# Hybrid decoder block on one core: the second norm's rows are turned by VectorE in 32x32 squares instead of by TensorE

## The chip, the core and the metric

The kernel runs on one core of a Trainium2 chip. The core has five engines, each with its own in-order stream of instructions: TensorE (PE: matrix products, with PEld for its weight loads), VectorE (DVE), ScalarE (ACT), GpSimd (POOL) and SyncE (SP), which here issues nearly all DMAs. Engines wait for one another, and for DMAs, by semaphores. The metric is the time of one execution on the device in microseconds; lower is better. In three runs the kernel before took 1904.53, 1905.38 and 1905.64 us, so its median is 1905.38 us.

## The reference, cut to what matters

One decoder layer on x of shape (1, 2048, 1024), all in float32:

```
h    = rmsnorm(x, norm_mix);  proj = h @ w_in            # 1024 x 2048
y    = concat(rmsnorm(rg_lru(conv4(...)) * gelu(...)), rmsnorm(silu(layernorm(conv31(...)))))
x    = x + y @ w_out
h    = rmsnorm(x, norm_ffn)                              # the second norm
f    = silu(h @ w_gate) * (h @ w_up)                     # hidden width 2816
x    = x + f @ w_down
out  = rmsnorm(x, norm_final)
```

The change concerns the line `h = rmsnorm(x, norm_ffn)` and how its result reaches the products with w_gate and w_up. TensorE contracts over the partition axis, so h, which is computed with positions on the partitions, must be turned so that its 1024 channels lie on the partitions.

## The kernel before, in words

Precision: every float32 operand is split in a high part (`_hi`) and a rest (`_lo`), and each product is three matmuls (lines 2133 to 2135): hi by hi, lo by hi, hi by lo. The split is a cast by ACT followed by a subtraction, by POOL for some operands and by DVE for others.

Stage 1 (to about 425 us) does the first norm, the input projection, the convolutions and the recurrence. It is not touched.

Stage 2, the **row steps** (425 to 624 us): 16 steps w = 0 to 15, each for 128 positions. In step w TensorE makes the output projection: four products `ps[e]` of twelve matmuls (`wo_hi`, `y_hi`, ...), 48 in all. Between them come a few short matmuls for the norms of later positions. DVE adds the four results to the residual in `row[w % 4]` (`add_row`, line 1729). ACT then takes the row's mean square and its root (`row_std`, lines 1351 and 1352), and DVE scales the row to `hn[w % 2]` (`row_scaled`, lines 1896 and 1903). PE, a little later, turns `hn` with eight 128x128 transposes into the banks 6 and 7 (`turn_h2`, line 2312); ACT copies them to `h2t` (`h2_copy`, line 1346), and SP stores `h2t` in the DRAM scratch `h2_scr` (`store_h2`, line 550), whose layout is channel by position. SP stores the row itself in `x2_scr` and loads later residuals and later y. The operand y of step w + 1 is cast by ACT (`y_split`, line 1260) and its rest is made by POOL (`y_lo_part`, line 888); PE's step waits for it (`pe.wait_ge(s_ylo, w + 1)`).

Stage 3 computes gate and up products by Strassen-like sums, for the first half of the positions (h = 0) and then for the second. Its left operands are seven tiles a0 to a6 (`a_raw`, split in `a_hi` and `a_lo`), each [128, 4 x 512]. For h = 0 four of them are loaded from `h2_scr` in row steps 9 and 10, and the others are sums made by DVE (`first_half_sum`, line 1874) in row steps 11 and 12. For step 14 POOL's program reads: the rest of y for step 14, the rest `b_lo` of the first weight matrix, a wait for the fourth sum (`s_sum0 >= 4`), the rest `a_lo` of a0, and only then the rest of y for step 15. The **hidden steps** i = 0 to 10 each take two weight matrices (m = 2i for gate, 2i + 1 for up), with seven products of twelve matmuls per matrix, n = 1, 2, 3, 4, 5, 0, 6. Product 2 waits for the rest `t_lo` of the matrix's sums by POOL, product 3 for DVE's sum `sum11` (line 1943). In hidden step i `sum11` of the gate matrix overwrites a part of the tile `gt`, and so it waits until operand 3 of step i - 1 (`f_scr<-gt`, line 685) is stored: `dve.wait_ge(s_fst[2], 16 * i)`. Operands of the down projection go to `f_scr`. For the second half SP loads parts of `h2_scr` into `quad` in the hidden steps 1, 3, 5 and 7, and POOL makes sums of them (`quad_sums`, line 987) in front of `t_lo` in its stream.

Stage 4 is the down projection; at its end DVE and ACT do the final norm on 16 row tiles `x2[t]`, and SP stores them.

The order of all this is written by hand, as tables of the step at which each piece stands (`TURNED`, `LOAD_AT`, `SUM_AT`, ...).

## Time and profile before

| | |
|---|---|
| median of three runs | 1905.38 us |
| the profiled execution, span of its instructions | 1902.7 us |
| PE busy | 1875.1 us, 99% |
| POOL, DVE, ACT busy | 60%, 58%, 42% |
| DMA | 284.20 MB, mean 149 GB/s |
| TensorE clock granted | full in all 40 slices |

The span is that of one execution; the timed median lies 2.7 us above it. Durations of matmuls in the profile overlap: 12 matmuls with a duration of 0.39 us each follow one another every 0.227 us. So PE's progress is read from start times, not from durations. The last row step, 15, ends at 624.1 us.

### The profile page before, as it was taken

Reading aid. Unit: us, or ns where it says so; the run is one execution under the profiler, and the core shown is the slowest. Engines: PE = TensorE matmul, PEld = TensorE weight load, DVE = VectorE, ACT = ScalarE, POOL = GpSimd, SP = SyncE. Lnnn points to the kernel's source line nnn. Section 1 sums busy time; section 2 is a strip of 40 time slices with the busy share of each in tenths; the row PEclk is TensorE's granted clock in tenths of the full one; section 3 lists DMA queues with packets and bytes.
Section 4 is the critical chain, followed back from the end, with each engine's and each line's share of the span. In section 5 each row is a group of like instructions: output and inputs, shape, how many; then the busy total and the mean of one; then the engine's idle time right before and its main releaser. Section 6 shows DMA issues by size and latency. Waiting matters only on the chain.

```text
span 1902.7 us, 22499 instructions
## 1 busy us (share of the span) xinstructions
PE 1875.1 (99%) x8374; PEld 1544.2 (81%) x8374; DVE 1106.6 (58%) x1269; ACT 808.4 (42%) x938; POOL 1144.9 (60%) x427
## 2 busy tenths in 40 slices
PE   9999999999999999999999999999999999999998
PEld 7888788877788788888888788888888888888886
DVE  6899988997645755455545854445443025433535
ACT  6466766585643533333333433333333222232235
POOL 3577477945734465666655755555555676676663
PEclk9999999999999999999999999999999999999999
DMA  6222132265777334533355433323333765655455
GB/s 196 78 79 88 45 100 78 75 224 172 247 240 231 117 125 127 153 119 127 112 153 176 151 105 114 106 88 105 115 105 127 288 225 190 210 189 211 166 198 221
DMA packets 240946, 284.20 MB, mean 149 GB/s; under 512 B 12095, under 2 KB 166207, under 8 KB 240364
## 3 DMA queue, kind: packets, MB, share of 16 engines
q1 hardware_dynamic: 240874, 283.25, 44.8%
q8 instruction: 45, 0.74, 0.2%
q14 instruction: 25, 0.20, 0.0%
q10 hardware_dynamic: 2, 0.00, 0.0%
HBM read 200.90 MB, written 82.31 MB: 149 GB/s over the span
## 4 chain that ended last, share of the span: by engine, by line
PE 82%; POOL 6%; DVE 5%; ACT 2%; issue 2%; DMA 2%; POOLq 0%; SPq 0%; DVEq 0%; ACTq 0%
PE ps L2133 19%; PE ps L2135 19%; PE ps L2134 19%; PE acc L2133 8%; PE acc L2135 8%; PE acc L2134 8%; DVE a_lo L1863 1%; POOL nsq L877 1%; PE ps L2161 1%; DVE t_sum L1887 1%; POOL nsq L879 1%; POOL w_lo L804 1%; POOL f_lo L1018 0%; DVE wo_lo L1707 0%; POOL glu L827 0%
## 5 line engine op out<-in xcount | busy, mean ns | idle before, releaser
L933 POOL TENSOR_TENSOR t_lo<-t_sum,t_hi 128x2048 fp32r<-128x2048 f32 x44 | 205.6, 4674 | 165.3 <-ACT t_hi L1366 165.2
L927 POOL TENSOR_TENSOR b_lo<-m_raw,b_hi 128x1536 fp32r<-128x1536 f32 x44 | 157.6, 3582 | 179.2 <-ACT b_hi L1361 121.9
L1018 POOL TENSOR_TENSOR f_lo<-f_raw,f_hi 128x2048 fp32r<-128x2048 f32 (+1 forms) x42 | 182.2, 4338 | 129.3 <-ACT f_hi L1518 124.8
L2133 PE MATMUL ps<-h_hi,w_hi 128*128 128x512 f32 x512 | 201.1, 393 | 0.8 <-POOL w_lo L804 0.8
L2135 PE MATMUL ps<-h_hi,w_lo 128*128 128x512 f32 x512 | 199.4, 389 | 0.0
L2134 PE MATMUL ps<-h_lo,w_hi 128*128 128x512 f32 x512 | 199.2, 389 | 0.0
L1887 DVE TENSOR_TENSOR t_sum<-m_raw 128x512 f32<-128x512 f32 x88 | 141.7, 1630 | 97.4 <-PE acc L2135 87.6
L1518 ACT CAST f_hi<-f_raw 128x2048 fp32r<-128x2048 f32 (+1 forms) x42 | 74.3, 1769 | 263.6 <-PE ps L2135 168.1
L2133 PE MATMUL ps<-wd_hi,f_hi 128*128 128x512 f32 x462 | 179.8, 389 | 0.8 <-POOL wd_lo L1025 0.8
L2134 PE MATMUL ps<-wd_lo,f_hi 128*128 128x512 f32 x462 | 179.7, 389 | 0.0
L2135 PE MATMUL ps<-wd_hi,f_lo 128*128 128x512 f32 x462 | 179.7, 389 | 0.0
L2076 DVE TENSOR_TENSOR wd_raw<-wd_raw 128x1024 f32<-128x1024 f32 (+1 forms) x30 | 73.6, 2453 | 174.8 <-DMA wd_raw<-in_w_down 174.8
L2133 PE MATMUL ps<-a_hi,t_hi 128*128 128x512 f32 x440 | 171.5, 390 | 0.8 <-DVE p5s L1959 0.8
L2134 PE MATMUL ps<-a_lo,t_hi 128*128 128x512 f32 x440 | 171.2, 389 | 0.0
L2135 PE MATMUL ps<-a_hi,t_lo 128*128 128x512 f32 x440 | 171.2, 389 | 0.0
L2133 PEld LDWEIGHTS ps<-h_hi,w_hi 128*128 128x128 f32 x512 | 96.1, 188 | 20.8 <-POOL w_lo L804 1.2
L2135 PEld LDWEIGHTS ps<-h_hi,w_lo 128*128 128x128 f32 x512 | 96.1, 188 | 20.3
L2134 PEld LDWEIGHTS ps<-h_lo,w_hi 128*128 128x128 f32 x512 | 96.2, 188 | 19.6 <-issue 0.2
L2133 PE MATMUL acc<-a_hi,t_hi 128*128 128x512 f32 x264 | 103.7, 393 | 4.0 <-DVE gt L1959 2.4
L2133 PE MATMUL ps<-a_hi,b_hi 128*128 128x512 f32 x264 | 102.9, 390 | 4.2 <-DVE a_lo L1863 2.6
L2133 PE MATMUL ps<-wo_hi,y_hi 128*128 128x512 f32 x256 | 104.6, 409 | 2.3 <-DVE wo_lo L1707 1.0
L2134 PE MATMUL acc<-a_lo,t_hi 128*128 128x512 f32 x264 | 103.3, 391 | 0.0
(257 smaller groups left out, 4689.1 us busy)
## 6 DMA issues: line engine op xcount, KB each, us to landing
f_raw<-f_scr SPq DMA_DIRECT2D x35, 1024.0 KB, 4.9
wd_raw<-in_w_down SPq DMA_DIRECT2D x60, 512.0 KB, 6.6
f_scr<-fs SPq DMA_DIRECT2D x110, 256.0 KB, 2.1
m_raw<-in_w_gate SPq DMA_DIRECT2D x88, 256.0 KB, 3.9
m_raw<-in_w_up SPq DMA_DIRECT2D x88, 256.0 KB, 5.1
w_raw<-in_w_in SPq DMA_DIRECT2D x32, 512.0 KB, 5.3
f_scr<-gt SPq DMA_DIRECT2D x44, 256.0 KB, 2.0
xt<-in_x SPq DMA_DIRECT2D x16, 512.0 KB, 6.3
```

The lines of the kernel that those rows point to most:

```text
L804: g.tensor_tensor(w_lo[q % 2][:, :, :, :], w_raw[q % 2][:, :, :, :], f32(w_hi[q % 2][:, :, :, :]), ALU.subtract).then_inc(s_wlo, 1)
L877: g.tensor_tensor(into[:, 0:2], source[:, 0:2], source[:, 2:4], ALU.add).then_inc(s_fold, 1)
L879: g.tensor_tensor(into[:, 0], into[:, 0], into[:, 1], ALU.add).then_inc(s_fold, 1)
L927: g.tensor_tensor(b_lo[b][:, :, :, :], m_raw[b][:, 0:3], f32(b_hi[b][:, :, :, :]), ALU.subtract).then_inc(s_mlo, 1)
L933: g.tensor_tensor(t_lo[b][:, :, :, :], t_sum[b][:, :, :, :], f32(t_hi[b][:, :, :, :]), ALU.subtract).then_inc(s_mlo, 1)
L1018: g.tensor_tensor(f_lo[j % 3][:, 0:n], f_raw[j % 2][:, 0:n], f32(f_hi[j % 3][:, 0:n]), ALU.subtract).then_inc(s_dlo, 1)
L1518: a.copy(f_hi[j % 3][:, 0:n], f_raw[j % 2][:, 0:n]).then_inc(s_dhi, 1)
L1887: v.tensor_tensor(into, in0, in1, ALU.subtract).then_inc(s_t, 1)
L2076: v.tensor_tensor(raw[:, 0, 0:c1 - c0], raw[:, 0, 0:c1 - c0], raw[:, 1, 0:c1 - c0], WD[m][2]).then_inc(s_t, 1)
L2133: pe.matmul(bank, lhs[0](c), rhs[0](c), start=first, stop=False, skip_group_check=more)
L2134: pe.matmul(bank, lhs[0](c), rhs[1](c), start=False, stop=False, skip_group_check=more)
L2135: mm = pe.matmul(bank, lhs[1](c), rhs[0](c), start=False, stop=last, skip_group_check=more)
```

## The change

- The 128 transposes of PE and the 32 copies of ACT are gone, and so are the tiles `h2t`.
- DVE turns each scaled row in its place in the stream: one instruction for [128, 32 squares of 32] turns every 32x32 square in itself (`row_turned`). It writes to `turned[g]`, one tile for a group of four rows. In `turned` the partition says the position within a square's 32 and the channel within its 32, mixed by the squares' order, so positions within a block of 512 stand in another order from here on.
- `hn` has four buffers for rows 0 to 3.
- SP stores a group of four rows with four DMAs of 32 partitions each, 512 KB in runs of 512 bytes, at row steps 7, 9 and 12. The last group is halved: rows 12 and 13 at step 14, and rows 14 and 15 in hidden step 0, each with four DMAs of 256 KB in runs of 256 bytes (64 positions).
- The first half's quarters are loaded with four DMAs of 32 partitions each, in row steps 10 and 11 (before 9 and 10), and the sums stand in row steps 12 and 13 (before 11 and 12).
- The second half is copied in DRAM from `h2_scr` to the new scratch `h2n_scr` in hidden step 1 (four DMAs, 4 MB in all), and SP waits for the copies to land before it issues the first `quad` load.
- The rows' other order is undone where rows are loaded and stored: `x2` loads and `out` stores become four DMAs of 32 partitions each. Of the last four pieces two are issued by ACT.

On DVE, before, the sums of a1 to a6 (`a_raw<-a_raw`) around row steps 11 to 13:

```order
L1903 SCALAR_TENSOR_TENSOR hn_208<-row_188,rstd,g_row 128x1024
L1874 TENSOR_TENSOR a_raw_62<-a_raw_65,a_raw_66 128x2048
L1874 TENSOR_TENSOR a_raw_65<-a_raw_61,a_raw_65 128x2048
L1729 SCALAR_TENSOR_TENSOR row_185<-ps,rms,row_185 128x512 x4
L1896 RECIPROCAL rstd<-rstd 128x1
L1903 SCALAR_TENSOR_TENSOR hn_207<-row_185,rstd,g_row 128x1024
L1874 TENSOR_TENSOR a_raw_63<-a_raw_62,a_raw_61 128x2048
L1874 TENSOR_TENSOR a_raw_64<-a_raw_60,a_raw_63 128x2048
L1729 SCALAR_TENSOR_TENSOR row_186<-ps,rms,row_186 128x512 x4
```

On DVE, now, the same sums, around row steps 12 to 14 (`row_187` is the row of step 12):

```order
L1768 SCALAR_TENSOR_TENSOR row_187<-ps,rms,row_187 128x512 x4
L1937 RECIPROCAL rstd<-rstd 128x1
L1944 SCALAR_TENSOR_TENSOR hn_209<-row_187,rstd,g_row 128x1024
L1955 STREAM_TRANSPOSE turned_148<-hn_209 128x32x32
L1915 TENSOR_TENSOR a_raw_62<-a_raw_65,a_raw_66 128x2048
L1915 TENSOR_TENSOR a_raw_65<-a_raw_61,a_raw_65 128x2048
L1768 SCALAR_TENSOR_TENSOR row_188<-ps,rms,row_188 128x512 x4
L1937 RECIPROCAL rstd<-rstd 128x1
L1944 SCALAR_TENSOR_TENSOR hn_210<-row_188,rstd,g_row 128x1024
L1955 STREAM_TRANSPOSE turned_148<-hn_210 128x32x32
L1915 TENSOR_TENSOR a_raw_63<-a_raw_62,a_raw_61 128x2048
L1915 TENSOR_TENSOR a_raw_64<-a_raw_60,a_raw_63 128x2048
```

Each pair of sums now stands one row step later and behind a square transpose. POOL's order is the same in both kernels; there, around row step 14, it is:

```order
L888 TENSOR_TENSOR y_lo_168<-y_raw_156,y_hi_162 128x1024
L927 TENSOR_TENSOR b_lo_78<-m_raw_74,b_hi_76 128x1536
L938 TENSOR_TENSOR a_lo_53<-a_raw_60,a_hi_67 128x2048
L888 TENSOR_TENSOR y_lo_169<-y_raw_157,y_hi_163 128x1024
L938 TENSOR_TENSOR a_lo_54<-a_raw_61,a_hi_68 128x2048
```

`a_lo_53`, the rest of a0, still stands in front of `y_lo_169`, the rest of y for row step 15, and it still waits for the fourth sum.

On SP, before, at the end of the row steps and in the hidden steps 0 and 1:

```order
L663 DMA x_scr<-row_188 128x1024
L550 DMA h_scr<-h2t_145 1024x1x128
L550 DMA h_scr<-h2t_146 1024x1x128
L567 DMA m_raw_74<-in_w_gate 128x4x128 x4
L567 DMA m_raw_75<-in_w_up 128x4x128 x4
L685 DMA f_scr<-gt_86 128x512 x2
L685 DMA f_scr<-fs 128x512 x5
L567 DMA m_raw_74<-in_w_gate 128x4x128 x4
L567 DMA m_raw_75<-in_w_up 128x4x128 x4
L669 DMA quad<-h_scr 128x512 x4
L685 DMA f_scr<-gt_86 128x512 x2
```

On SP, now, the same stretch:

```order
L715 DMA x_scr<-row_190 128x1024
L617 DMA m_raw_74<-in_w_gate 128x4x128 x4
L617 DMA m_raw_75<-in_w_up 128x4x128 x4
L585 DMA h_scr<-turned_148 1024x1x64 x4
L734 DMA f_scr<-gt_86 128x512 x2
L734 DMA f_scr<-fs 128x512 x5
L617 DMA m_raw_74<-in_w_gate 128x4x128 x4
L617 DMA m_raw_75<-in_w_up 128x4x128 x4
L600 DMA h2n_scr<-h_scr 256x1024 x4
L718 DMA quad<-h2n_scr 128x512 x4
L734 DMA f_scr<-gt_86 128x512 x2
```

The store of the last turned rows moved behind the weight loads and stands directly in front of operand 3 (`f_scr<-gt`), and the copies in DRAM stand between the weight loads and the first `quad` load.

The diff, cut to its core:

```
-        TURNED = {3: (0, 1), 4: (2, 3)}
+        TURN_AT = {4: (0, 1), 5: (2,), 6: (3, 4), 7: (5,), 8: (6, 7)}
+        STORE_GROUP_AT = {7: 0, 9: 1, 12: 2}
+        STORED = 16 * SQS
-        LOAD_AT, SUM_AT = 9, (11, 12)
+        LOAD_AT, SUM_AT = 10, (12, 13)
...
+            def store_group(g):
+                h, st = divmod(g, NS)
+                sp_.wait_ge(s_turned, GROUP * (g + 1))
+                for t in range(SQS):
+                    cols = slice(st * TILE + t * P, st * TILE + (t + 1) * P)
+                    sp_.dma_start(h2_scr[h, :, :, :, cols].rearrange("j k q s -> j (k q) s"),
+                                  turned[g][t * SQ:(t + 1) * SQ]).then_inc(s_h2st[g], 16)
+            def store_last(half):
+                n = P // 2
+                sp_.wait_ge(s_turned, NT - 2 + 2 * half)
+                for t in range(SQS):
+                    first = (NS - 1) * TILE + half * 2 * P + t * n
+                    sp_.dma_start(h2_scr[NH - 1, :, :, :, first:first + n].rearrange("j k q s -> j (k q) s"),
+                                  turned[3][t * SQ:(t + 1) * SQ]).then_inc(s_h2st[3], 16)
+            def second_half_in_place():
+                for q in range(SQS):
+                    sp_.dma_start(h2n_scr[q * SQ:(q + 1) * SQ], h2_scr[1, :, :, q]).then_inc(s_h2n, 16)
...
                     next_matrices(h, i, i)
+                    if i == 0:
+                        store_last(1)
                     if i == QUADS[0]:
-                        for n in range(2):
-                            sp_.wait_ge(s_h2st[n], 16 * NT // 2)
+                        sp_.wait_ge(s_h2st[2], STORED)
+                        sp_.wait_ge(s_h2st[3], 2 * STORED)
+                        second_half_in_place()
+                        sp_.wait_ge(s_h2n, STORED)
...
-                if starts == 0:
-                    h2_copy(NT - 2)
...
+            def row_turned(w):
+                g, r = divmod(w, GROUP)
+                if w >= NT - 2:
+                    dve.wait_ge(s_h2st[3], STORED)
+                if g == NT // GROUP - 1:
+                    r = r % 2
+                dve.wait_ge(s_hn, w + 1)
+                v.transpose(turned[g][:, :, r * SQ:(r + 1) * SQ], hn[hb(w)][:, :].rearrange("p (b i) -> p b i", i=SQ)
+                            ).then_inc(s_turned, 1)
...
+                for r in TURN_AT.get(w, ()):
+                    row_turned(r)
                 if w == 1 or 3 <= w < NT - 2:
                     row_scaled(w)
+                if TPH <= w < NT - 2:
+                    row_turned(w)
...
                     f_sum(0, i, h, first and h == 0)
                     f_sum(1, i, h, first and h == 0)
+                    if first and h == 0:
+                        row_turned(NT - 2)
+                        row_turned(NT - 1)
...
-            def turn_h2(w):
-                pe.wait_ge(s_hn, w + 1)
-                for b in range(2):
-                    ...
-                    for k in range(4):
-                        c = (4 * b + k) * P
-                        mm = pe.transpose(ps[6 + b][:, k * P:(k + 1) * P], hn[w % 2][:, c:c + P], ident[:, :])
-                    mm.then_inc(s_tr[b], 1)
...
-                for turned in TURNED.get(w, (w - 1,) if 5 <= w < NT - 1 else ()):
-                    turn_h2(turned)
```

## Rows read from the trace of the kernel before

**Rows 1.** The page's first part: busy us (share of the span) x instructions.
```profile
PE 1875.1 (99%) x8374; PEld 1544.2 (81%) x8374; DVE 1106.6 (58%) x1269; ACT 808.4 (42%) x938; POOL 1144.9 (60%) x427
```

**Rows 2.** Timeline, PE: start us, duration us, engine, line, operation, tiles, count [idle before <-releaser].
```profile
469.82 1.04 PE L2312 MATMUL ps<-ident,hn 128*128 128x128 f32 x8
...
472.38 0.39 PE L2134 MATMUL ps<-wo_lo,y_hi 128*128 128x512 f32 x1
...
500.69 1.04 PE L2312 MATMUL ps<-ident,hn 128*128 128x128 f32 x8
...
501.81 0.39 PE L2134 MATMUL ps<-wo_lo,y_hi 128*128 128x512 f32 x1
```

**Rows 3.** Timelines of POOL and PE before row step 8.
```profile
514.04 2.41 POOL L877 TENSOR_TENSOR nsq<-nsq 128x1024 f32<-128x1024 f32 x1 [3.46 <-ACT nsq L1121]
...
528.68 0.50 PE L2133 MATMUL ps<-wo_hi,y_hi 128*128 128x512 f32 x1 [0.64 <-POOL y_lo L888]
```

**Rows 4.** Timeline, PE, hidden step 0.
```profile
638.67 0.50 PE L2133 MATMUL ps<-a_hi,b_hi 128*128 128x512 f32 x1 [2.63 <-DVE a_lo L1863]
```

**Rows 5.** Timelines of PE, DVE, ACT and POOL, row steps 12 to 15.
```profile
588.77 1.03 PE L2312 MATMUL ps<-ident,hn 128*128 128x128 f32 x8
...
613.14 0.48 PE L2133 MATMUL ps<-wo_hi,y_hi 128*128 128x512 f32 x1
...
588.15 2.71 DVE L1729 SCALAR_TENSOR_TENSOR row<-ps,rms,row 128x512 f32<-128x512 f32 x4
...
592.61 1.28 DVE L1903 SCALAR_TENSOR_TENSOR hn<-row,rstd,g_row 128x1024 f32<-128x1024 f32 x1
593.81 4.61 DVE L1874 TENSOR_TENSOR a_raw<-a_raw,a_raw 128x2048 f32<-128x2048 f32 x2
...
595.89 1.48 ACT L1361 CAST b_hi<-m_raw 128x1536 fp32r<-128x1536 f32 x1
...
600.75 3.50 POOL L927 TENSOR_TENSOR b_lo<-m_raw,b_hi 128x1536 fp32r<-128x1536 f32 x1
604.21 5.59 POOL L938 TENSOR_TENSOR a_lo<-a_raw,a_hi 128x2048 fp32r<-128x2048 f32 x1
609.77 2.39 POOL L888 TENSOR_TENSOR y_lo<-y_raw,y_hi 128x1024 fp32r<-128x1024 f32 x1
```

**Rows 6.** Timelines of DVE and POOL at 633 us.
```profile
633.05 5.57 DVE L1863 TENSOR_TENSOR a_lo<-a_raw,a_hi 128x2048 fp32r<-128x2048 f32 x1
...
632.97 3.50 POOL L927 TENSOR_TENSOR b_lo<-m_raw,b_hi 128x1536 fp32r<-128x1536 f32 x1 [3.98 <-ACT b_hi L1361]
```

**Rows 7.** Timelines of SP, DVE and PE, hidden steps 0 and 1.
```profile
662.83 10.04 SPq L685 DMA_DIRECT2D f_scr<-gt  x2
...
672.52 1.29 DVE L1984 TENSOR_TENSOR fs<-gt 128x512 f32<-128x512 f32 x2 [5.55 <-POOL gt L976]
...
674.24 0.39 PE L2133 MATMUL ps<-a_hi,t_hi 128*128 128x512 f32 x1
...
676.96 0.39 PE L2133 MATMUL acc<-a_hi,t_hi 128*128 128x512 f32 x1
```

**Rows 8.** DMA from 614.5 to 623 us, 40 slices: GB/s; then KB, us to landing.
```profile
GB/s 0 0 0 14 277 282 292 294 287 299 284 294 145 0 0 0 0 0 0 0 0 0 0 0 0 0 0 0 0 0 0 0 0 0 0 0 0 0 0 0
...
h_scr<-h2t SPq DMA_DIRECT2D x1, 512.0 KB, 3.5
```

**Rows 9.** Timelines of POOL and DVE, hidden steps 1 and 2.
```profile
697.96 3.45 POOL L987 TENSOR_TENSOR quad<-quad 128x512 f32<-128x512 f32 x2
702.28 4.60 POOL L933 TENSOR_TENSOR t_lo<-t_sum,t_hi 128x2048 fp32r<-128x2048 f32 x1 [0.86 <-ACT t_hi L1366]
...
712.90 0.69 DVE L1943 TENSOR_TENSOR gt<-y2s,acc 128x512 f32<-128x512 f32 x1 [0.67 <-PE acc L2135]
```

**Rows 10.** Windows: stretch, its us, busy us of PE, PEld, DVE, ACT, POOL, PE clock, DMA share, GB/s.
```profile
1070.00:1080.00 10.00, 7.60 (x27) 5.81 (x26) 10.00 (x10) 5.40 (x6) 5.19 (x1) 0.83 0.51 162
```

**Rows 11.** Timeline, SP, the last store of the kernel.
```profile
1899.48 0.45 SPq L782 DMA_DIRECT2D out_block<-x  x1
```

More of the change, by code:

```diff
@@ L155, in hybrid_block @@
         ones = at("ones", [P, P], F32, 196 * KIB + 384)
-        hn = [at(f"hn{s}", [P, D], F32, (208 + 4 * s) * KIB) for s in range(2)]
+        hn = [at(f"hn{s}", [P, D], F32, o * KIB) for s, o in enumerate((208, 212, 200, 116))]
         junk = at("junk", [P, D], BF16, 216 * KIB)
@@ L335, in hybrid_block @@
         s_downf = sem("down_read")
-        s_x2ld = [sem(f"x2_loaded{r}") for r in range(2)]
+        s_x2ld = [sem(f"x2_loaded{n}") for n in range(3)]
         s_fsq = sem("final_row_ready")
@@ L418, in from_sbuf, with hb, pieces, out_piece @@
             return m, nd[m][:, :, first * P:(first + 1) * P]
+        def hb(w):
+            return w if w < 4 else w % 2
+        def pieces(t):
+            block, a = divmod(t, GROUP)
+            if block < NT // GROUP - 1:
+                return [(GROUP * block + r, SQ * a) for r in range(GROUP)]
+            return [(GROUP * block + 2 * (a // 2) + r, SQ * (2 * (a % 2) + n)) for n in range(2) for r in range(2)]
+        def out_piece(t, n):
+            w, p = pieces(t)[n]
+            return outr[w][p:p + SQ, :]
         def decay_of(u):
@@ L1117, in norm_swish @@
                     y_split(between)
-                if turned is not None:
-                    h2_copy(turned)
                 act.wait_ge(s_ysw, NJ * (m + 1))
@@ L1564, in _ @@
             a.activation(last_row[:, TILE:D], last_row[:, TILE:D], ACT.Copy, scale=rstd[:, NT - 1:NT]).then_inc(s_std2, 1)
+            act.wait_ge(s_std2, 2 * NT + 2)
+            act.wait_ge(s_fsq, NT + 2)
+            for n in range(2, SQS):
+                a.dma_start(out_piece(row_tile(NB - 1, 0), n), last_row[n * SQ:(n + 1) * SQ, :]).then_inc(s_ost, 16)
         @block.vector
@@ L2370, in _ @@
                     norm_var(1, 6)
-                for turned in TURNED.get(w, (w - 1,) if 5 <= w < NT - 1 else ()):
-                    turn_h2(turned)
             BANKS = [[ps[4], ps[5], ps[0], ps[5], ps[0], ps[5], ps[5]], [ps[4], ps[1], ps[0], ps[1], ps[0], ps[1], ps[1]]]
```

117 lines of the change are left out of this document (55 added, 62 removed).

## The prediction

> **What bounds the kernel now.** I read four things. The page's first part comes first: PE is busy for 1875.1 of 1902.7 us, and no other engine is above 60% [rows 1]. So time comes out only where PE's own work goes, or where PE waits less, and time goes in wherever PE has to wait anew. Second, PE's timeline around each turn, to see what a turn costs PE and what PE would wait for in its place [rows 2 to 4]. Third, the waits at the end of the row steps, where the fourth sum, the rest of a0 and the rest of y for step 15 follow one another; there I compare DVE, ACT and POOL with PE's start of each step [rows 5, 6]. Fourth, SP's stream in the hidden steps 0 to 2, since stores and copies are moved in front of transfers that somebody needs [rows 7 to 9].
>
> **What the change takes from PE.** Eight transposes start at 469.82 and the next matmul after two such turns starts at 472.38. Matmuls follow one another every 0.227 us anyway, so two turns cost 2.56 − 0.23 = 2.33 us [rows 2]. There are two such pairs: 4.7 us. A single turn goes from 500.69 to 501.81 and costs 1.12 − 0.23 = 0.89 us [rows 2]. There are ten such, at the ends of the steps 5 to 14, but not all come through. Row step 8 started at 528.68 after waiting 0.64 us for POOL's `y_lo` [rows 3]. POOL had been at work without a pause from 514.04 on, when ACT's squares released it. That chain, which starts from y that is loaded, does not get shorter within these steps, so the three turns at the ends of the steps 5, 6 and 7 give nothing; the pairs before them I let come through, since the chain's start moves with them. The seven later ones, the ends of steps 8 to 14, give 7 x 0.89 = 6.2. The turns of rows 14 and 15 stand in hidden step 0, where PE waits for DVE's `a_lo` anyway: 2.63 us of idle time end at 638.67 [rows 4]; they give 0.1. Removed: 4.7 + 6.2 + 0.1 = **−11.0**. The ends are −14 (all ten singles count) and −6 (the chain swallows the pairs too).
>
> **ACT's copies.** They go (32), and PE waits for none of them. Nothing is counted.
>
> **The square transposes on DVE.** The trace has no such instruction. The nearest row by size is DVE's scaling of the same 1024 elements per partition, 1.28 us [rows 5]; I take that, with 1.1 and 2.6 as the ends (the second: twice the row). Sixteen of them are 20 us of DVE, but DVE is 58% busy [rows 1] and in most steps waits for the root from ACT, so they cost nothing where the next thing on DVE is not late. They count at two places, below.
>
> **Row step 14.** DVE adds row 12 from 588.15, 0.6 us before PE has ended the step (588.77), because it came out of two sums just then [rows 5]. Now the first pair of sums stands behind the scaling and a transpose of that same row (+1.3), and the step is 0.9 us shorter. So the next adds begin about 1.6 us too late for the banks, less some slack: **+1.0** (0 to 2.2).
>
> **Row step 15.** This is the largest term. POOL's order is b_lo, wait for the fourth sum, a_lo of a0, y_lo of step 15. Before, the sums ended about 598.4 (593.81 + 4.61), 9.6 us after PE's end of step 12; y_lo ended at 612.16 and PE began step 15 at 613.14 [rows 5]. The margin was 1 us. Now the sums stand a whole step later, while PE's wish to begin step 15 comes earlier. Counting from PE's end of step 13: the adds end at +2.2 (590.86 is 2.1 after 588.77); root, scaling take 2.95 until 593.81; the transpose 1.3; the two sums 4.6: +11.1. But ACT's cast `b_hi` releases POOL's `b_lo` about 6.5 us after the adds' end (595.89 + 1.48 against 590.86), and beside a running POOL instruction of 3.50 us DVE's 2048-element subtraction took 5.57 us against 4.61/2 = 2.3 for a sum of the same size with POOL quiet [rows 5, 6]. I add 3.5 for that overlap: the fourth sum at +14.6. Then a_lo 4.6 (5.59 with overlap [rows 5]) and y_lo 2.4: +21.6. PE wants to start at +11.1 (a step is 48 matmuls, 48 x 0.227 = 10.9, and I allow 0.2 for a gap). Stall: 10.5 us; without the overlap 7. After such a pause PE runs at half clock for a while: in a window of 10 us where PE was busy for 7.60 us, the granted clock was 0.83 [rows 10], which is 3.4 us at 1.2 instead of 2.4 GHz and so 1.7 us lost. **+12.2** (7 to 14).
>
> **Hidden step 1.** SP's store of operand 3, `f_scr<-gt`, now stands behind the store of rows 14 and 15. That one waits for the 16th transpose, and the last two transposes stand on DVE behind the sums `fs`, which took from 672.52 to 673.8 [rows 7]: 2 x 1.28 later, at 676.4, is the latest. But SP's loads of matrix 2 no longer stand behind the stores of the last rows, and this can bring the whole chain to `fs` forward by 2 us (an estimate); I take 674.3 to 676.3 for the four issues. Its 1 MB goes in runs of 256 bytes: 4096 packets. Before, 512 KB in runs of 512 bytes (1024 of them) took 3.5 us with issue, and at 285 GB/s alone [rows 8] one such packet costs one of the 16 DMA engines 512 x 16 / 285,000 = 0.029 us. If the packet, and not the byte, is the price, 4096 / 16 x 0.0275 = 7.0 us; if the byte, 3.7. I take 7.0, since the store with the short runs (512 KB in 3.5 us) was slower than its bytes at 285 GB/s (1.8). The packets are through at about 681.8; operand 3, 512 KB behind them, lands about 2.5 later at 684.3, and `sum11`, which overwrites it, ends at 685.0. Product 3 follows product 2 after 2.72 us (674.24 to 676.96 [rows 7]) and so wants to start at 677.2. Stall 7.8, and again 1.7 for the clock: **+9.5** (1.9 to 17).
> The Trainium skill ("DMA: Bandwidth & Descriptors", section "Specifications") says that transfers below 512 bytes fall under line rate, since the engine reads, modifies and writes; taken as twice the time per packet it is an estimate of 14 us for this store instead of 7, and the stall would be 15. No row of this trace has runs of 256 bytes in a store.
>
> **Hidden step 2.** The copy in DRAM is issued behind the matrices of hidden step 1's turn on SP, at about 690 to 694.5, and moves 4.19 MB. If a byte counts once at the 285 GB/s of [rows 8] it takes 14.7 us, if each is paid twice 29; it could also be faster, as this kernel shows no such copy, and I let it down to 10. I take 17. The weights issued just before it are on the way for some 4 us more, so it lands about 694.5 + 4 + 17 = 715.5. The `quad` parts follow, 1 MB: 3.7 by bytes, 1.7 for the way as in the store of [rows 8] (3.5 against 1.8), and 0.9 of issue: 721.8. POOL adds them (3.45) and makes t_lo (4.60) [rows 9]: 729.9; before, t_lo ended at 706.88 (702.28 + 4.60). Product 3 needed `sum11`, whose end was 713.6 (712.90 + 0.69), some 6 us behind t_lo (712.9): now 735.9. Its plan is 676.96 + 14 x 2.72 = 715.0, with 9.5 of the stall before 724.5. **+11.4** (3 to 20); the clock is not added, since a part of this wait falls at product 2, which is also late (729.9 against 721.8).
> The Trainium skill ("SBUF — State Buffer", section "Door 1: The DMA port swizzle (why [64,N] ≈ [32,N])") says that 32 partitions reach only 8 of 16 ports and gives 189 GB/s for them against 328 for 128 partitions. Group stores and quarter loads, all of 32 partitions each, would by that take an estimated 11 us per 2 MB where they run alone, unless four of them side by side cover all ports; loads of y in the row steps 9 to 13 would be late by 4 to 5 us, and the time an estimated 1934. No row here shows a bulk transfer of 32 partitions.
>
> **The end.** The last store is one piece in 0.45 us of SP, issued at 1899.48 [rows 11]. Two DMAs on SP and two on ACT add one issue and a landing: **+0.6** (0.3 to 1).
>
> **Sum.** −11.0 + 1.0 + 12.2 + 9.5 + 11.4 + 0.6 = +23.7. The profiled execution of before spans 1902.7 us, so the same of the changed kernel would span 1926.4. The median of the timed runs stands 2.7 us above the span, which I keep: 1905.4 + 23.7 = 1929.1, so **1929.0**.
>
> **Rivals.**
> A is this forecast: three new waits, each behind a thing that was moved later.
> B: only the hand-over of step 15 holds in full; the small packets go by the byte (hidden step 1: 1.9) and the copy is at its fast end (3.0). For it speaks that DMA moved 162 GB/s in a stretch of the hidden steps [rows 10], so there is room. Against it: the runs are half as long as any before, and the copy must be finished in whole before the first `quad` load. −11.0 + 1.0 + 12.2 + 1.9 + 3.0 + 0.6 = +7.7, time 1913.
> C: narrow DMAs and short runs are both dear. The store takes twice the packet price (stall 15 + 1.7), the copy pays each byte twice (20), and y or the weights in row steps 9 to 13 come late by 4.3. −11.0 + 1.0 + 12.2 + 16.7 + 20 − 1.5 (clock time counted once for both) + 4.3 + 0.6 = +42, time 1947. For it speaks that the stores of both kernels are bound by something else than bytes (0.5 MB in 3.5 us [rows 8]); against it that the DMA engines were busy for 0.51 of such a stretch [rows 10].
> D, the other side: the rest of y for step 15 is in time, and the turn's absence comes through. It decides at one point: y_lo of step 15 has to end within 10.9 us of PE's end of step 13, and for that the fourth sum must end by +4 (before: +9.6 from the step before it). It would need the sums to run while POOL still has its rest of y in front, which the order does not show. −11.0 + 0 + 0 + 1.9 + 3.0 + 0.6 = −5.5, time 1900.
> That the change does not do what it says is excluded by the order: PE has no transposes of `hn` left, and DVE has 16 square ones.
>
> **Numbers.** A has a chance of 0.60, B 0.17, C 0.15, D 0.08. Differences under 0.2%, 3.8 us, can't be told from none. A and C are slower; of B, 0.10 is slower and 0.07 falls within 0.2% (the stall of step 15 at its lower end, 7, and no clock loss: +1); of D, 0.06 is faster and 0.02 the same. So faster 0.06, same 0.09, slower 0.85. The range reaches from below B, 1911, to C, 1948; A's own is 1918 to 1940.
>
> **What would show it.** In the profile of the changed kernel: row steps 9 to 13 apart by 10.9 us instead of 11.8 (removed turns). A POOL row `a_lo` starting only after the second pair of DVE sums, `y_lo` right behind it, and PE idle for about 10 us before step 15, released by POOL's `y_lo`. In hidden step 1 PE idle before product 3, released by DVE's `sum11`, which itself waits for operand 3's store; if instead that wait is under 3 us, the price of short runs is wrong. In hidden step 2 PE waits for `t_lo` or `sum11` behind POOL's `quad` sums, and POOL waits for DMA. The square transpose should stand at 1.1 to 2.6 us. The prediction fails as a whole if PE starts step 15 without a wait, or if the `quad` loads land before 712.

## The result, and the profile after

The changed kernel takes 1930.67 us (median of four runs, 1926.66 to 1931.30), the kernel before 1904.95 us beside it (1904.26 to 1905.64): ratio 1.0128, 95% interval 1.0114 to 1.0142. It is 1.3% slower. The profiled executions span 1928.7 and 1902.7 us: 26.0 us apart, where the prediction had 23.7.

The page's first part, after; busy us (share of the span) x instructions:

```profile
PE 1873.4 (97%) x8246; PEld 1538.4 (80%) x8246; DVE 1119.2 (58%) x1285; ACT 792.6 (41%) x906; POOL 1143.7 (59%) x427
```

Against [rows 1], PE has 128 instructions fewer, DVE 16 more, ACT 32 fewer. PE's share fell because it waits more. The view of PE's waits, after (what waited, released by whom: us in total, times, longest):

```profile
PE ps L2194 <- POOL y_lo L944: 14.3, 4, 6.3
PE acc L2194 <- DVE gt L1999: 8.2, 2, 6.8
PE ps L2194 <- POOL t_lo L989: 3.7, 1, 3.7
PE ps L2194 <- DVE a_lo L1902: 3.5, 1, 3.5
```

Before, the wait for `y_lo` was one of 0.6 us [rows 3]. PE's timeline, after, at six places:

```profile
523.05 0.50 PE L2194 MATMUL ps<-wo_hi,y_hi 128*128 128x512 f32 x1 [2.88 <-POOL y_lo L944]
...
597.47 0.79 PE L2194 MATMUL ps<-wo_hi,y_hi 128*128 128x512 f32 x1 [4.72 <-POOL y_lo L944]
...
617.26 0.79 PE L2194 MATMUL ps<-wo_hi,y_hi 128*128 128x512 f32 x1 [6.34 <-POOL y_lo L944]
...
690.70 0.79 PE L2194 MATMUL acc<-a_hi,t_hi 128*128 128x512 f32 x1 [6.84 <-DVE gt L1999]
...
731.85 0.61 PE L2194 MATMUL ps<-a_hi,t_hi 128*128 128x512 f32 x1 [3.71 <-POOL t_lo L989]
...
737.81 0.50 PE L2194 MATMUL acc<-a_hi,t_hi 128*128 128x512 f32 x1 [1.38 <-DVE gt L1999]
```

These are, from the top, row steps 8, 14 and 15, product 3 of hidden step 1, and products 2 and 3 of hidden step 2. The same work of PE set side by side, after minus before, gives the account: in each row the start of the same instruction before and after (the last matmul of row step 13, the first of matrix 0, and so on; DVE's last scaling in the row before the last), and by how much the distance between the two kernels grew in that stretch.

| Stretch, to its end | at, before and after | measured | forecast |
|---|---|---|---|
| up to the last matmul of row step 13 | 600.31, 592.36 | −8.0 | −9.2 |
| row steps 14 and 15 | 624.12, 630.87 | +14.7 | +11.4 |
| hidden step 0 | 674.24, 680.97 | 0.0 | 0 |
| hidden step 1 | 679.68, 695.33 | +8.9 | +9.5 |
| hidden step 2 | 725.92, 748.82 | +7.2 | +11.4 |
| the rest, to the last scaling by DVE | 1898.36, 1922.76 | +1.5 | 0 |
| the last stores | span 1902.7, 1928.7 | +1.6 | +0.6 |

(In the forecast column the 11.0 us for the turns are split: 9.2 up to step 13, 1.8 in steps 14 and 15.) The largest thing that the sum had not counted is the wait of row step 14. The waits and transfers in front of it, after, on DVE and ACT, then POOL:

```profile
590.59 4.62 DVE L1915 TENSOR_TENSOR a_raw<-a_raw,a_raw 128x2048 f32<-128x2048 f32 x2 [4.24 <-DMA a_raw<-h_scr]
...
591.86 1.05 ACT L1314 CAST y_hi<-y_raw 128x1024 fp32r<-128x1024 f32 x1 [8.30 <-DMA y_raw<-d_scr]
...
593.00 4.42 POOL L944 TENSOR_TENSOR y_lo<-y_raw,y_hi 128x1024 fp32r<-128x1024 f32 x1 [11.47 <-ACT y_hi L1314]
606.93 3.50 POOL L983 TENSOR_TENSOR b_lo<-m_raw,b_hi 128x1536 fp32r<-128x1536 f32 x1 [9.52 <-ACT b_hi L1405]
610.39 4.51 POOL L994 TENSOR_TENSOR a_lo<-a_raw,a_hi 128x2048 fp32r<-128x2048 f32 x1
614.86 2.34 POOL L944 TENSOR_TENSOR y_lo<-y_raw,y_hi 128x1024 fp32r<-128x1024 f32 x1
```

The first three say that y for step 14 and the quarters for the sums both came late from DMA, and that `y_lo` ran for 4.4 instead of 2.4 us beside DVE's sums. The last three are the queue that the prediction named: b_lo, a_lo, y_lo, and PE starts step 15 at 617.26, right behind.

But what held this queue up is not what the prediction named. `a_lo` has no wait: it starts as soon as `b_lo` has ended. POOL's idle time of 9.52 us stands in front of `b_lo`. The second pair of sums on DVE, and ACT's casts:

```profile
602.08 4.58 DVE L1915 TENSOR_TENSOR a_raw<-a_raw,a_raw 128x2048 f32<-128x2048 f32 x2
...
599.26 3.69 ACT L1400 CAST a_hi<-a_raw 128x2048 fp32r<-128x2048 f32 x2
605.37 1.49 ACT L1405 CAST b_hi<-m_raw 128x1536 fp32r<-128x1536 f32 x1 [2.42 <-DMA m_raw<-in_w_gate]
606.87 1.06 ACT L1314 CAST y_hi<-y_raw 128x1024 fp32r<-128x1024 f32 x1
```

The fourth sum had ended at 606.66, before `b_lo` began at 606.93. What was late is ACT's cast `b_hi`: it stands behind the root of row 13 and the casts of a0 and a1, and it waited 2.42 us more for the first weight matrix.

Why DMA was late shows in the windows (stretch, its us, busy us of PE, PEld, DVE, ACT, POOL, PE clock, DMA share, GB/s), from 566 to 582 us, within row steps 10 to 12. Before:

```profile
566.00:582.00 16.00, 16.00 (x78) 13.32 (x76) 6.33 (x10) 5.77 (x11) 2.40 (x1) 1.00 1.07 353
```

After:

```profile
566.00:582.00 16.00, 15.68 (x70) 12.68 (x69) 6.94 (x9) 2.50 (x4) 4.11 (x2) 1.00 1.09 254
```

The DMA engines are busy all the time in both, but they moved 353 GB/s before and 254 after (the transfers in the stretch are not the same ones). In hidden steps 0 to 2, SP and DVE, after:

```profile
680.77 3.83 SPq L585 DMA_DIRECT2D h_scr<-turned  x4
684.65 3.17 SPq L734 DMA_DIRECT2D f_scr<-gt  x2
...
700.66 2.71 SPq L600 DMA_DIRECT2D h2n_scr<-h_scr  x4
718.23 1.76 SPq L718 DMA_DIRECT2D quad<-h2n_scr  x4
...
678.38 2.36 DVE L1955 STREAM_TRANSPOSE turned<-hn 128x1024 f32<-128x1024 f32 x2
...
689.96 0.69 DVE L1999 TENSOR_TENSOR gt<-y2s,acc 128x512 f32<-128x512 f32 x1 [7.91 <-DMA f_scr<-gt]
```

`sum11` (L1999) waits 7.9 us for the store of operand 3, which stands behind the last rows' store. The `quad` loads are issued only at 718.2, when the copy has landed.

### The profile page after: what moved, and what is told of

Its sections match the earlier page's. It is cut to its first block, busy times and chain, and to the rows that moved or that the text cites. A ratio compares the mean times of both kernels' runs of the same rounds, so it can differ in the third digit from the quotient of the medians.

```text
span 1928.7 us, 22315 instructions
## 1 busy us (share of the span) xinstructions
PE 1873.4 (97%) x8246; PEld 1538.4 (80%) x8246; DVE 1119.2 (58%) x1285; ACT 792.6 (41%) x906; POOL 1143.7 (59%) x427
## 4 chain that ended last, share of the span: by engine, by line
PE 74%; POOL 8%; DVE 6%; DMA 4%; issue 3%; ACT 2%; SPq 2%; POOLq 0%; DVEq 0%; ACTq 0%
PE ps L2194 17%; PE ps L2196 17%; PE ps L2195 17%; PE acc L2194 7%; PE acc L2195 7%; PE acc L2196 7%; DMA wd_raw<-in_w_down 1%; POOL f_lo L1074 1%; DVE a_lo L1902 1%; DVE t_sum L1928 1%; DMA y_raw<-d_scr 1%; POOL nsq L933 1%; POOL y_lo L944 1%; POOL wd_lo L1081 1%; SPq L594 1%
## 5 line engine op out<-in xcount | busy, mean ns | idle before, releaser
L2194 PE MATMUL ps<-wo_hi,y_hi 128*128 128x512 f32 x256 | 106.3, 415 | 15.9 <-POOL y_lo L944 14.3
```

What stands on the lines that cost most here:

```text
L2194: pe.matmul(bank, lhs[0](c), rhs[0](c), start=first, stop=False, skip_group_check=more)
```

## Experiments

Ratios are to the kernel before on the same chip, with 95% intervals; its median was 1907.2 us beside the first four kernels, 1906.8 beside the next four, 1905.4 beside the three after them and 1906.4 beside the last. "From m0 to m5" is the time on PE from the first product of matrix 0 to the second product of matrix 5, which holds hidden steps 0 to 2: 101.8 us before and 118.0 after. Matrix 0 starts at 624.12 before and at 630.87 after. The profiled executions are single ones, and they drift apart before any edit acts: row step 8 starts at 523.05 in the changed kernel, 523.10 in y_first and 526.13 in wide_loads, whose programs are the same up to there. So stretches in the row steps are also given from the start of step 8 to matrix 0: 95.4 us before, 107.8 after.

**no_turn: what PE's turns cost by themselves** (an edit of the kernel before; it leaves the turning out, so its products are not the reference's)

```
-                    act.wait_ge(s_tr[b], w + 1)
-                    a.copy(h2t[w % 2][...], ps[6 + b]...)
+                    act.wait_ge(s_hn, w + 1)
+                    a.copy(h2t[w % 2][...], hn[w % 2][...]...)
...
-                    turn_h2(turned)
```

> The kernel before with PE's 128 transposes of hn left out; ACT copies the unturned hn to h2t instead of the bank, everything else as before (what the hidden stage multiplies is then not the turned rows). It asks what PE's turns cost by themselves. Theory: two pairs at 2.33 us and the seven singles of steps 8 to 14 at 0.89 give 11.0 us, while the wait for y_lo before step 8 grows from 0.64 to about 3.3 us: about 1894. Rival 1: the y_lo chain swallows the pairs too: 6 us, about 1899. Rival 2: nothing is swallowed: 14 us, about 1891.

Measured: 1897.19 us, 0.9952 (0.9935 to 0.9969), 10.0 us under before; matrix 0 starts at 612.33, 11.8 earlier. The wait for `y_lo` in row steps 8 and beyond is 2.4 us in total. The forecast of 11.0 fits, and so does the size of what is swallowed: all turns together are 13.7 us by the prediction's prices, and 11.8 arrive at matrix 0. The interval, 6 to 12 us saved, shuts out rival 2 (14) but touches rival 1 (6); against rival 1 speaks the start of matrix 0. Which turns are swallowed was not tested one by one. So the removal had about the worth that was forecast, and the loss is in the rest of the change.

**y_first: the rest of y for step 15 in front of a_lo**

```
-                if w > 4:
+                if w > 4 and w < NT - 1:
                     y_lo_part(w)
                 if w == NT - 2:
                     raw_lo(0, 0)
+                    y_lo_part(NT - 1)
                     pool.wait_ge(s_sum0, 4)
                     a_low(0)
```

> The changed kernel with one move on POOL: the rest of y for step 15 stands in front of the wait for the fourth sum and of a_lo of a0, instead of behind. Theory: PE's 6.34 us before step 15 are the a_lo and the sums in front of y_lo. Then y_lo ends behind b_lo (610.4 + 2.4 = 612.8) and PE waits 1.9 us there; with some of the half clock behind it gone too, 4.5 to 6.5 us less: 1924 to 1926. Rival: y itself, or the cast b_hi behind a late weight load, is what comes late in step 15, and the move gives under 2 us: about 1930. The 4.7 us before step 14 stay in both.

Measured: 1927.61 us, 1.0108 (1.0091 to 1.0125). That misses the 1924 to 1926 and lies between theory and rival; the median is 3.1 us under the changed kernel's, and the intervals overlap, so the times alone do not show a gain. The rows do. POOL and PE:

```profile
605.49 3.50 POOL L983 TENSOR_TENSOR b_lo<-m_raw,b_hi 128x1536 fp32r<-128x1536 f32 x1 [10.35 <-ACT b_hi L1406]
608.94 2.34 POOL L944 TENSOR_TENSOR y_lo<-y_raw,y_hi 128x1024 fp32r<-128x1024 f32 x1
...
611.34 0.50 PE L2195 MATMUL ps<-wo_hi,y_hi 128*128 128x512 f32 x1 [2.79 <-POOL y_lo L944]
```

The wait before step 15 falls from 6.34 to 2.79 us, and the clock stays up (granted 1.00 from 605 to 625 us, 0.83 in the changed kernel). What went is `a_lo`'s own 4.5 us in front of `y_lo`. The 2.8 us that stay are `b_hi`, which here waited 3.25 us for the weight matrix: the rival's cause is there as well. Matrix 0 starts at 622.36, but from m0 to m5 it is 120.1 us instead of 118.0, so a part of the gain is waited for again in the hidden steps.

**wide_loads and wide_both: are DMAs of 32 partitions slow?**

```
-                for q in range(SQS):
-                    sp_.dma_start(a_raw[n][q * SQ:(q + 1) * SQ], h2_scr[0, :, ..., q, ...])
+                for k in range(KH):
+                    sp_.dma_start(a_raw[n][:, k], flat[:, half * KH + k, ...])   # flat: [128, 8, 1024]
```

> The changed kernel with the first half's four quarters loaded as 128 partitions per DMA instead of 32: the same number of DMAs (16), the same 256 KB each, the same runs of 2 KB, but read from h2_scr as if it lay partition by partition, so that the values stand in another order than the reference wants. It asks whether breadth in partitions makes the DMA engines slow in row steps 9 to 13 (216 to 229 GB/s at full share, where before had 350 to 390). Theory (breadth): the loads run at 300 to 390 GB/s again, the 1 MB quarter lands in under 6 us, a_raw is there before the sums (no 4.2 us of DVE), y for step 14 comes in time, and PE's 4.7 us before step 14 shrink to under 1.5: about 1924 to 1926. Rival (the stores with runs of 512 bytes in 32 partitions, or sheer bytes, are what fills the queues): 0 to 1 us less.

> As wide_loads, and the stores of row groups 0 to 2 too: still four DMAs of 512 KB with runs of 512 bytes per group, but 128 partitions in each (again values in another order). Theory (breadth): all of row steps 7 to 13 runs at the rate of before; PE's wait before step 14 is gone and the half clock behind it too, and y_lo of step 15 waits only for the sums: 1921 to 1924. Rival (runs of 512 bytes cost by themselves): no more gain than wide_loads has.

Measured: 1929.00 us, 1.0111 (1.0092 to 1.0130), and 1925.81 us, 1.0112 (1.0093 to 1.0131). Both leave the values in another order than the reference wants. The window of row steps 10 to 12, of wide_loads:

```profile
560.00:582.00 22.00, 22.00 (x99) 18.22 (x98) 11.21 (x15) 4.77 (x8) 5.54 (x2) 1.00 1.04 353
```

And its longest wait of PE behind that, before step 15 (the waits of 590 to 625 us):

```profile
PE ps L2194 <- POOL y_lo L944: 9.6, 1, 9.6
```

The changed kernel moved 265 GB/s in the same window. Same bytes, same number of DMAs, same runs of 2 KB, but 128 partitions instead of 32: breadth is what the transfers lack. (With the breadth the edit also changes the order in which the runs are read from DRAM; no run changed that alone.) The wait before step 14 is gone in both kernels, but the time hardly moves: both expectations, 1924 to 1926 and 1921 to 1924, are missed, and neither interval is clear of the changed kernel's. From step 8 to matrix 0 they take 104.1 and 103.3 us instead of 107.8. The wait before step 15 has grown from 6.3 to 9.6 us. In these kernels the hand-over of step 15 stands alone, and no DMA is late in it; the prediction had 10.5. POOL and DVE in wide_loads:

```profile
604.11 5.53 POOL L983 TENSOR_TENSOR b_lo<-m_raw,b_hi 128x1536 fp32r<-128x1536 f32 x1 [13.69 <-ACT b_hi L1405]
609.59 4.50 POOL L994 TENSOR_TENSOR a_lo<-a_raw,a_hi 128x2048 fp32r<-128x2048 f32 x1
...
601.76 4.58 DVE L1915 TENSOR_TENSOR a_raw<-a_raw,a_raw 128x2048 f32<-128x2048 f32 x2
```

Here too `a_lo` starts without a wait, and the fourth sum had ended at 606.34, before `b_lo` did. This pair of sums cost POOL only what it added to `b_lo` beside it, 5.53 instead of 3.50 us.

The Trainium skill ("SBUF — State Buffer", section "Door 1: The DMA port swizzle (why [64,N] ≈ [32,N])") gives 189 GB/s for partitions 0 to 31 against 328 for all 128. The trace agrees in kind: from 560 to 582 us most slices with these loads stand at 186 to 238 GB/s in the changed kernel, and in wide_loads most with wide ones at 331 to 439.

**store_after: the last rows stored behind the operands**

```
                     next_matrices(h, i, i)
-                    if i == 0:
-                        store_last(1)
...
                     store_f(h, i, i)
+                    if i == 0:
+                        store_last(1)
```

> The changed kernel with the store of rows 14 and 15 moved on SP from in front of operand 3 to behind the operands of hidden step 0. Theory: the wait before product 3 of hidden step 1 (6.8 us, and 1.9 of half clock) is operand 3 stuck behind that store; it goes, 8 to 9 us less: about 1922, if the copy in hidden step 1 does not wait longer for the last rows. Rival 1: the two square transposes behind the sums on DVE hold up sum11 themselves: 2 to 3 us stay. Rival 2: the freed time is waited for again at t_lo of m = 4, since the quad loads come no earlier: only 1 to 3 us less in the end, about 1928.

Measured: 1928.82 us, 1.0115 (1.0098 to 1.0132), from m0 to m5 118.0 us as before the edit. The wait of hidden step 1 is gone (product 3 starts at 682.66, 2.72 behind product 2), and PE pays it in hidden step 2:

```profile
730.85 0.79 PE L2194 MATMUL ps<-a_hi,t_hi 128*128 128x512 f32 x1 [11.38 <-POOL t_lo L989]
```

11.38 us instead of 3.71, at nearly the same time (731.85 in the changed kernel). The expected 1922 is missed. Rival 2 of this expectation is right: the copy lands when it lands, and two waits in a row were one debt paid in two parts.

**no_copy: the quad parts straight from the squares' order**

```
-                        second_half_in_place()
-                        sp_.wait_ge(s_h2n, STORED)
...
-                    sp_.dma_start(quad[:, n], quarter(a)[:, k])
+                    sp_.dma_start(quad[:, n], h2_scr[1, :, half * KH + k, :, ...].rearrange("j q s -> q j s"))
```

> The changed kernel without the copy in DRAM: each quad part and each later quarter of the second half is loaded straight from h2_scr, with 128 partitions in a DMA whose partition steps through the squares' order; the quad parts are four DMAs as now. Theory: hidden step 2's waits (3.7 at product 2, about 3.3 at product 3) are the copy in front of the quad loads; they go, 7 us less: 1923.5. Rival: the waits are POOL's quad sums, which stand in front of t_lo in every case, and stay: about 1930. How long the copy took is read from the changed kernel's DMA beside this one's.

Measured: 1944.53 us, 1.0193 (1.0174 to 1.0212), the slowest of all, 21 us above the expectation. Hidden step 2 has no wait (from m0 to m5: 110.3), but PE waits 6.3 and 9.1 us at the start of the second half (at 1066.7 and 1081.0), behind ACT's casts of quarters loaded in the same way. DMA from 701 to 711 us, 40 slices: share in tenths, GB/s:

```profile
DMA  9999999999999999932222222222222222222222
GB/s 348 309 295 293 291 293 287 289 291 291 291 291 291 287 279 248 229 125 66 98 98 90 98 90 106 98 98 107 107 106 98 98 98 106 98 98 98 107 107 106
```

Once the weights are through and the quad loads alone are under way, the share falls to two tenths and the rate to about 100 GB/s: a DMA whose outermost step has four entries uses a quarter of the engines. The Trainium skill ("DMA: Bandwidth & Descriptors", section "🔬 Why a DMA increments its semaphore by 16 and not by 1") says that the number of engines is the largest one up to 16 that divides the slowest dimension of both access patterns, here 4; these rows agree. The expectation had not weighed it.

**narrow_quads: the same, with four DMAs of 32 partitions each**

```
-                    sp_.dma_start(quad[:, n], quarter(a)[:, k])
+                    for q in range(SQS):
+                        sp_.dma_start(quad[q * SQ:(q + 1) * SQ, n], h2_scr[1, :, half * KH + k, q, ...])
```

> The changed kernel without the copy in DRAM, as no_copy, but each quad part is loaded by four DMAs of 32 partitions (16 of 64 KB per group), and each later quarter too. no_copy's quad loads moved 100 GB/s at a fifth of the engines' share, since its outermost step had four entries. Theory: with 32 entries outermost all 16 engines work, the first quad group lands at about 711 instead of 721, and PE's 7 us in hidden step 2 go: 1923 to 1925. Rival: SP needs 0.5 us for each of 16 issues per group, so operands behind them come late, and of the 7 us less than 3 are won: 1928 and more.

Measured: 1924.87 us, 1.0096 (1.0079 to 1.0112), as expected; from m0 to m5 110.2 us. The 7 us of hidden step 2 are the copy's: without it PE has no wait there. SP takes 8.61 us for the 16 issues and nobody waits for it.

**fix_orders: y_first, store_after and narrow_quads together**

> y_first, store_after and narrow_quads together: computes what the reference wants. Theory: store_after alone won nothing since the copy's landing held PE in hidden step 2 at the same time in any case; with the copy gone too, the 16 us of hidden steps 1 and 2 come back in full, and y_first's 4 to 5: 1930.7 - 16 - 4.5 = 1910. Rival: the last rows' landing (4.4 us behind four issues) or POOL's quad sums still hold up t_lo of m = 4: 3 to 6 us stay, 1913 to 1916.

Measured: 1915.90 us, 1.0048 (1.0030 to 1.0066); from m0 to m5 105.5 us, which is 12.5 of the 16.2 that were lost. It misses the 1910 and lies at the rival's end. What stays in the hidden steps is one wait of 1.6 us for `sum11` (721.52) and 3.8 for `a_lo` where before had 2.6 [rows 4], with clock. In the row steps the waits before steps 14 (3.77) and 15 (4.38) stay.

**m0_first, two_queues, two_queues2: three tries at the row steps** (each on top of the one before it, the first on fix_orders; two_queues2 also issues ACT's loads one row step later than two_queues does)

```
+                if w == LOAD_AT + 2:
+                    load_matrix(0)
                 if w in STORE_GROUP_AT:
                     store_group(STORE_GROUP_AT[w])
...
+                        for q in (2, 3):
+                            a.dma_start(a_raw[n][q * SQ:(q + 1) * SQ], ...)      # on ACT
...
+                    for t in (2, 3):
+                        a.dma_start(h2_scr[h_, ...], turned[g_][t * SQ:(t + 1) * SQ])   # on ACT
```

> fix_orders, and on SP the first weight matrix is loaded before the store of row group 2 (which holds SP for 11 us) instead of behind it. In y_first and fix_orders PE still waits 2.8 us for y_lo of step 15, with ACT's cast of y for step 15 queued behind its cast b_hi, and b_hi waiting for that matrix. Theory: b_hi is early, y_hi and y_lo of step 15 too, and that wait falls under 1 us: 2 to 3 us less than fix_orders, about 1913. Rival: the load for y of step 15, also behind the group store on SP, is as late as the matrix was: no change, and the earlier matrix only crowds y of step 14 more (wait 4.4 before step 14 grows).

> m0_first, and of each quarter of the first half ACT issues the two DMAs of partitions 64 to 127, while SP issues those of partitions 0 to 63, so that two DMAs for different partitions are under way side by side. Theory (32 partitions at a time reach only a part of the ways into the on-chip memory): the rate in row steps 10 to 12 rises from about 220 to over 280 GB/s, and PE's wait of 4.4 us before step 14 shrinks to under 2: about 1909 to 1911. Rival (each DMA engine takes the rows of 32-partition DMAs one after another whatever the queue): no gain, within 1 us of m0_first.

> two_queues, and of the stores of row groups 0 to 2 ACT issues two of four DMAs too. Theory: stores and loads both run side by side, another 1 to 2 us less: about 1908, near the kernel before (1906.8 on the same chip). Rival: ACT now waits for DVE's transposes in its own order and the casts of y behind are late: slower than two_queues by 1 to 4 us.

Measured: 1916.39 us, 1.0052 (1.0036 to 1.0069); 1920.03 us, 1.0076 (1.0059 to 1.0093); 1914.36 us, 1.0047 (1.0030 to 1.0064). None is clear of fix_orders (1.0030 to 1.0066; two_queues, the slowest, only just meets it), and all three expectations, 1913, 1909 to 1911 and 1908, are missed. In m0_first the matrix comes early, and ACT now waits for y itself, as the rival said:

```profile
605.32 1.47 ACT L1412 CAST b_hi<-m_raw 128x1536 fp32r<-128x1536 f32 x1
610.94 1.05 ACT L1321 CAST y_hi<-y_raw 128x1024 fp32r<-128x1024 f32 x1 [4.14 <-DMA y_raw<-d_scr]
```

In two_queues ACT's own wait for the group stores, in front of its loads, holds up a cast of y, and PE pays for it. ACT, then PE:

```profile
562.19 1.04 ACT L1321 CAST y_hi<-y_raw 128x1024 fp32r<-128x1024 f32 x1 [12.02 <-issue]
...
565.71 0.79 PE L2211 MATMUL ps<-wo_hi,y_hi 128*128 128x512 f32 x1 [6.96 <-POOL y_lo L950]
```

So two_queues does not test the second queue by itself. In two_queues2, with the loads one step later, this wait is not there, and the rival (slower than two_queues) is wrong: it is 5.7 us faster. From 560 to 582 us the three moved 264, 282 and 290 GB/s, each with somewhat different transfers in the stretch. At most, two queues side by side give narrow transfers a little, not what breadth gives (353 in wide_loads, 371 in wide_all).

**wide_all: fix_orders with wide stores and loads in the row steps**

> fix_orders with the stores and the loads of wide_both (128 partitions in each DMA in row steps 7 to 13, so the values stand in another order than the reference wants). It asks whether three orders (y_lo behind a_lo, the last store in front of operand 3, the copy in front of the quad loads) and narrow DMAs are the whole loss. Theory: the waits before row steps 14 and 15 go (8 us and some 4 of half clock), what is left of the change is the turns' 8 to 10 us against about 3 in the hidden steps, 1.5 at the half of stage 3 and 1.6 at the end: 2 to 5 us faster than the kernel before, 1900 to 1904. Rival: there is a cost in the row steps that none of these four explains (DVE's transposes, or the sums a step later): the hidden stage starts no earlier than 620 and the time stays at 1907 or more.

Measured: 1911.74 us, 1.0028 (1.0016 to 1.0039). The values are again in another order. The rival is right: something stays. Matrix 0 starts at 623.27, 98.6 us after step 8; in no_turn, with only the turns gone, it is 612.33 and 89.8. DVE, ACT, POOL and PE before step 15:

```profile
587.91 5.54 DVE L1922 TENSOR_TENSOR a_raw<-a_raw,a_raw 128x2048 f32<-128x2048 f32 x2
593.36 2.72 DVE L1775 SCALAR_TENSOR_TENSOR row<-ps,rms,row 128x512 f32<-128x512 f32 x4
...
597.50 3.71 ACT L1407 CAST a_hi<-a_raw 128x2048 fp32r<-128x2048 f32 x2
601.12 1.47 ACT L1412 CAST b_hi<-m_raw 128x1536 fp32r<-128x1536 f32 x1
602.49 1.04 ACT L1321 CAST y_hi<-y_raw 128x1024 fp32r<-128x1024 f32 x1
...
602.66 5.53 POOL L989 TENSOR_TENSOR b_lo<-m_raw,b_hi 128x1536 fp32r<-128x1536 f32 x1 [13.69 <-ACT b_hi L1412]
608.15 2.34 POOL L950 TENSOR_TENSOR y_lo<-y_raw,y_hi 128x1024 fp32r<-128x1024 f32 x1
...
610.54 0.80 PE L2201 MATMUL ps<-wo_hi,y_hi 128*128 128x512 f32 x1 [5.16 <-POOL y_lo L950]
```

There is one more order. The step at which ACT casts a0, a1 and the first matrix hangs on `LOAD_AT`, so it moved from row step 12 to 13 with the loads, and now the three casts stand right in front of y of step 15 on ACT, and `b_lo` (5.5 us beside DVE's sums) in front of `y_lo` on POOL. The casts in turn stand behind the root of row 13, whose additions on DVE (593.36) stand behind the first pair of sums, and that pair behind the square transpose of row 12. So the sums and the transposes moved onto this chain too. That this chain is all of the 5.2 us is read from the rows; a kernel with these casts placed elsewhere was not run.

## Why the prediction was right, and where it was not

It forecast 1929.0 us; 1930.7 was measured. The nearness is in part luck: terms are off by up to 6 us, on both sides. Row step 14 cost 7.2 us (4.7 of wait and 2.5 of half clock) where 1.0 was forecast, and row step 15 and hidden step 2 cost some 3 and 4 us less than forecast.

- **The turns, −11.0.** no_turn measures −10.0 in the median, with an interval of some 6 to 12. Up to step 13 the changed kernel gains 8.0 where 9.2 was forecast: step 8 waits 2.88 instead of 0.64 us, as said, and runs on the lower clock behind it (from 500 to 530 us the granted clock is 0.94, with 1.00 before). The same wait does not always bring the lower clock: in y_first step 8 waits 2.87 us and the same window shows 1.00.
- **The square transposes.** 1.20 to 1.25 us each, 1.28 forecast. No wait is put down to them in the row steps, but each stands in front of the sums on DVE.
- **Row step 14, +1.0.** The term was mis-sized: it counted only DVE's late row addition. Measured are 4.7 us of wait for `y_lo`, by late DMAs, and 2.5 of half clock behind it (1.0 against 7.2). The prediction had this in its sentence on the 32 partitions and in rival C at 4.3 us, and left it out of the sum.
- **Row step 15, +12.2.** The place, the order on POOL (b_lo, a_lo, y_lo) and the size were right; the link between them was wrong. The prediction let `a_lo` wait for the fourth sum at +14.6 us after PE's end of step 13, and laid the cost of the overlap (3.5) on the sums. wide_loads, where no DMA is late, has the fourth sum at +11.3, as it would be without overlap; the overlap fell on `b_lo` (+2.0), and it is `b_lo` that ends at +14.6. In no trace here does `a_lo` wait for a sum where it stands in front of `y_lo`. So the 9.6 us of wait against the 10.5 forecast are right in size and partly by luck. `b_hi` is in its forecast place in wide_loads, 6.5 us after the row's additions; that this figure holds ACT's casts, moved with `LOAD_AT`, was not named as an order of its own. In the changed kernel `b_lo` begins 5.6 us later than forecast (+14.3 for +8.7): 3.1 by additions that stand behind the late first sums, 2.4 by the late weight matrix. y_first shows the part of the order itself: without `a_lo` in front the wait is 2.8 instead of 6.3. 6.3 us of wait and 2.7 of half clock were paid here, 9.0 against 12.2, since step 14 had already paid for a part. Steps 14 and 15 together came to 14.7 against 11.4.
- **Hidden step 1, +9.5.** Measured 8.9, at product 3, released by `sum11`, which waited for operand 3's store. The reason given for the price, 256-byte runs, is not shown. Its evidence was that 512 KB took 3.5 us where its bytes take 1.8; but the term for hidden step 2 counts the same 1.7 us as the way to landing, and it can't be both. (The working also has 0.029 us per packet and then 0.0275, worth 0.3 us.) The 1 MB moved mostly at 178 to 228 GB/s, and loads with runs of 2 KB in 32 partitions moved at the same 186 to 238, so breadth alone may explain it. No run stored 256-byte runs from 128 partitions. The Trainium skill's rule ("DMA: Bandwidth & Descriptors", section "Specifications"), which gives no factor, was taken as twice the time per packet and would so have made the wait 15 us; with 6.8 measured the trace does not agree with that factor.
- **Hidden step 2, +11.4.** Measured 7.2, so the copy was priced too high. Each of its four DMAs landed 11.8 us (median) after issue, all four by 718.2, 17.5 us after the first issue; the term had 25.5 (690 to 715.5). From 700 to 718 us, 5.35 MB in all were moved, the copy's 4.19 MB among them, so a byte counts once; most slices stand at 300 to 446 GB/s, above the 285 of [rows 8].
- **The steps are not a sum.** store_after and wide_loads each took one wait away and won nothing clear of the noise: what was late behind it took all of its place in store_after, and nearly half of it in wide_loads (the wait before step 15 grew by 3.3 us). The prediction's terms added up because each was worked out with the ones before it in place; as savings they do not add.
- **The end, +0.6.** Measured 1.6: SP's last two issues take 1.84 us and begin at 1924.48, behind the four stores of the piece before them, where before one issue of 0.45 stood at 1899.48 [rows 11]. The 1.5 us between hidden step 2 and the end (1.1 of it a new wait for DVE's `y2s` near the middle of stage 3) were not forecast.

No version of the change here beats the kernel before. Taking three orders and the narrow transfers of the row steps away still leaves 0.28% over the kernel before (0.16 to 0.39%), so the turns' own 10 us are still spent elsewhere.

## What to carry to other kernels

When a step of a hand-written order is moved by one, list every engine's instructions that hang on the same number: here the loads, the sums and ACT's casts moved together, and the casts came to stand in front of a y that PE needed. When a queue is late, look at which of its members has the idle time in front of it: the wait that the program writes down (here for the fourth sum) need not be the one that holds. Before you remove one wait, ask which landing holds the next one: if a later landing holds PE anyway, removing the earlier wait alone wins nothing (store_after), while removing the later one did (narrow_quads, 7.8 us from m0 to m5). Rearranging through DMA by groups of 32 partitions cost rate here where the DMA engines were busy all the time (254 against 353 GB/s); count it from the GB/s of slices whose share is at its top, not from bytes.
